# A hybrid decoder trunk in split single precision: first-half sum and second-half high parts moved at the changes of sub-layer

## What is computed

```python
def decoder_layer(x, state, norm_gains, ...):
    g = norm_gains
    x = x + 0.5 * rmsnorm(swiglu(rmsnorm(x, g[0]), ffn1_w_gate, ffn1_w_up, ffn1_w_down), g[1])
    mix, new_state = token_mixer(rmsnorm(x, g[2]), state, w_in, ..., w_out)
    x = x + rmsnorm(mix, g[3])
    x = x + 0.5 * rmsnorm(swiglu(rmsnorm(x, g[4]), ffn2_w_gate, ffn2_w_up, ffn2_w_down), g[5])
    return x, new_state
```

## Time and profile before

| | |
|---|---|
| Runs | 2288.12, 2284.45, 2284.33 us; median 2284.45 |
| Profiled execution | 2289.84 us, its span 2287.8 us |
| Mean granted TensorE clock | 0.986 of full speed |
| PE busy | 2223.0 us (97%), 19753 matmuls |
| DVE / ACT / POOL busy | 908.3 / 790.3 / 946.3 us |
| Chain that ended last | PE 92%, DVE 4%, ACT 2%, POOL 1%, issue 1% |
| DMA | 191.95 MB, 29.6% of the 16 engines' span |

### The profile page before, as it was taken

One profiled execution on the slowest core, in us unless ns is written; L12 is line 12 of the kernel. 1 busy time (PEld: TensorE's weight loads), 2 busy tenths in 40 slices (PEclk: granted clock), 3 DMA queues, 4 the chain that ended last, 5 costly groups with the idle time before them and its releaser, 6 DMA issues.

```text
span 2287.8 us, 45399 instructions
## 1 busy us (share of the span) xinstructions
PE 2223.0 (97%) x19753; PEld 2168.6 (95%) x19753; DVE 908.3 (40%) x1366; ACT 790.3 (35%) x1466; POOL 946.3 (41%) x781
## 2 busy tenths in 40 slices
PE   7999999999999999999999999999999999999998
PEld 7999999899888899999999999999998889999998
DVE  6333311666346733321263332135654556333113
ACT  4333322433343533332253333234143435333222
POOL 3644444433224444444444444434333344444442
PEclk9999999999999999999999999999999999999999
DMA  3333322322233233323223333323223132333232
GB/s 119 93 89 88 100 88 82 81 66 62 57 88 91 76 95 88 88 83 92 83 82 88 88 88 100 88 77 72 68 55 96 51 105 81 88 88 88 82 92 69
DMA packets 386181, 191.95 MB, mean 84 GB/s; under 512 B 31344, under 2 KB 384896, under 8 KB 385984
## 3 DMA queue, kind: packets, MB, share of 16 engines
q1 hardware_dynamic: 385984, 189.06, 29.6%
HBM read 180.26 MB, written 8.75 MB: 83 GB/s over the span
## 4 chain that ended last, share of the span: by engine, by line
PE 92%; DVE 4%; ACT 2%; POOL 1%; issue 1%; DMA 0%; SPq 0%; ACTq 0%
PE ps L771 84%; PE ps L993 1%; DVE xn_lo L1779 1%; DVE x L1793 1%; PE ps L1242 1%; POOL proj L755 1%; PE ps L929 1%; DVE numer L2169 0%; DVE y_ffn L1789 0%; ACT w_hi L1312 0%; DVE acc L1772 0%; ACT xn_hi L1323 0%; PE ps L1098 0%; PE ps L1139 0%; PE ps L1127 0%
## 5 line engine op out<-in xcount | busy, mean ns | idle before, releaser
L686 POOL TENSOR_TENSOR w_lo<-w_raw,w_hi 128x512 fp32r<-128x512 f32 (+1 forms) x680 | 881.9, 1301 | 1303.8 <-ACT w_hi L1312 1302.1
L771 PE MATMUL ps<-xn_hi,w_hi 128*128 128x272 f32 x3904 | 863.7, 295 | 32.3 <-DVE xn_lo L1779 25.2
L771 PE MATMUL ps<-xn_hi,w_lo 128*128 128x272 f32 x3904 | 846.9, 291 | 0.0
L771 PE MATMUL ps<-xn_lo,w_hi 128*128 128x272 f32 x3904 | 845.4, 290 | 0.0
L1312 ACT ACTIVATE w_hi<-w_raw 128x512 fp32r<-128x512 f32 (+1 forms) x680 | 415.1, 614 | 1073.8 <-PE ps L771 1018.8
L771 PEld LDWEIGHTS ps<-xn_hi,w_hi 128*128 128x128 f32 x3904 | 633.3, 191 | 57.8 <-DVE xn_lo L1779 31.4
L771 PEld LDWEIGHTS ps<-xn_lo,w_hi 128*128 128x128 f32 x3904 | 634.5, 191 | 0.2
L771 PEld LDWEIGHTS ps<-xn_hi,w_lo 128*128 128x128 f32 x3904 | 631.1, 191 | 0.0
L771 PE MATMUL ps<-h_hi,w_hi 128*128 128x272 f32 x1344 | 291.7, 288 | 0.0
L771 PE MATMUL ps<-h_lo,w_hi 128*128 128x272 f32 x1344 | 291.0, 287 | 0.0
L771 PE MATMUL ps<-h_hi,w_lo 128*128 128x272 f32 x1344 | 290.9, 287 | 0.0
(11 more groups left out here) (316 smaller groups left out, 1367.5 us busy)
## 6 DMA issues: line engine op xcount, KB each, us to landing
w_raw<-in_ffn_w_gate SPq DMA_DIRECT2D x168, 256.0 KB, 2.8
w_raw<-in_ffn_w_up SPq DMA_DIRECT2D x168, 256.0 KB, 2.8
w_raw<-in_ffn_w_down SPq DMA_DIRECT2D x160, 256.0 KB, 2.8
w_raw<-in_w_in SPq DMA_DIRECT2D x120, 256.0 KB, 2.8
w_raw<-in_w_out SPq DMA_DIRECT2D x32, 256.0 KB, 2.9
s_c<-in_state_mlstm_C SPq DMA_DIRECT2D x8, 512.0 KB, 6.1
out_c_s<-s_c SPq DMA_DIRECT2D x8, 512.0 KB, 5.9
tok_in<-in_x_prompt SPq DMA_DIRECT2D x4, 512.0 KB, 4.2
```

Source lines behind the costliest of these rows:

```text
L686: pool.tensor_tensor(w_lo[:, n % RING, 0:m], w_raw[:, n % RAW, 0:m], w_hi[:, n % RING, 0:m].bitcast(F32), ALU.subtract).then_inc(w_split, 1)
L771: mm = pe.matmul(pair(p)[:, a, :], w[:, q, ws], z[:, k, half(a)], start=(k == 0 and w is w_hi and z is hi), stop=(k == chunks - 1 and w is ...
```

## The change

Three edits, all of order; no instruction is added or removed.

```diff
@@ pe_ffn, closing: behind block 0 of the second half, no longer block 1
-                    if a == 1 and b == 1:
+                    if a == 1 and b == 0:
                         pe_post_sum(pe, v, 0)
@@ pe_mix, closing: inside the loop over blocks b, behind b == 0
+                        if a == 1 and t == DC - 3 and b == 0:
+                            pe_post_sum(pe, v, 0)
...
-                    if a == 1 and t == DC - 3:
-                        pe_post_sum(pe, v, 0)
@@ act_open
             act_x_square(act, 3)
+            act_x_high(act, v, 1, 5)
             act_high(act, n + 6)
-            act_x_high(act, v, 1, 5)
-            act_x_square(act, 4)
+            act_x_high(act, v, 1, 6)
             act_high(act, n + 7)
-            act_x_high(act, v, 1, 6)
-            act_x_square(act, 5)
             act_x_high(act, v, 1, 7)
             act_high(act, n + 8)
+            act_x_square(act, 4)
+            act_x_square(act, 5)
             keep_raw(1, 0)
@@ act_turn_from_ffn and act_turn_from_mix, the same edit in both
             act_high(act, n)
+            act_post(act, u, 0)
             act_high(act, n + 1)
-            act_post(act, u, 0)
```

## The result

| | before | with the change |
|---|---|---|
| Median | 2288.70 us (14 runs, 2284.33 to 2292.00) | 2278.11 us (14 runs, 2270.22 to 2282.57) |
| Ratio | | 0.9948, 95% interval 0.9939 to 0.9957 |
| Profiled execution | 2289.84 us, span 2287.8, mean granted clock 0.986 | 2282.23 us, span 2279.7, clock 0.986 |
| PE waits for a low part of x | 25.2 us, 22 times | 18.0 us, 14 times |

Faster by half a per cent, which the interval tells from no change; the forecast was 2276.0. The median of before over fourteen runs is 4.2 us above that of the three runs which the prediction had.

A forecast was written before the change was run, and what follows sets the result against it. PE, busy 97% of the span, idles 65 us; at the changes it waits for DVE's low part of x, held by POOL's splits. Terms of 9.9 us less idle: 2284.45 - 9.9 + 1.5 = 2276.0 us; range 2272 to 2279, with rivals 2271.5 to 2284.0.

The forecast's parts named there:

- rival B: At the three changes from an FFN POOL wins the 0.12 us tie: 2.7 us less won, 2278.7 us; chance 0.24.
- a split holds DVE off for about 1.05 us: POOL's split and a DVE operation on two SBUF tensors take turns, each split holding DVE off about 1.05 us.
- closing, three changes from an FFN: First halves after an FFN: earlier sum, Ln and Exp bring chunk 3's low part 1.1 us sooner each, 3.3 in all.
- closing, two from the mixer: First halves at the two changes that leave the mixer: the earlier sum wins 0.3 us each, 0.6 in all.
- opening, two with memsets: Second halves from FFN to mixer: memsets leave chunk 7's low part unheld, 1.9 us each, 3.8 in all.
- opening, the other three: Second halves of the other three changes: the split of n+7 holds chunk 7's low part; 0.6 us each, 1.8 in all.
- first opening: Opening of the first sub-layer: by the same reasoning as the other openings, 0.4 us won.
- rival E: The edits do nothing for PE because transfers or the ring are just behind: 2284 us; chance 0.06.
- I charge one more slow place, 1.5: Two pauses melted into one may slow more places to 1.2 GHz; 1.5 us added to the time.
- Rival D: Slower: melted pauses at six such places and two mixer first halves all run at 1.2 GHz, 2287.3 us; chance 0.09.
- the cover stays: Pre-norm sum in the openings: DVE still finishes about 2 us before PE asks for it.
- C (absorbed): DVE and POOL absorb the gain in first halves and openings without memsets; 4.2 us remain, 2280.3 us; chance 0.16.

The follow-up runs named there:

- The shorter splits: The whole change, but POOL splits only 128 of 512 columns of blocks n+1 to n+5 at each change; 2263.83 us, ratio 0.9875 to the kernel before.
- the last set of profiles: Kernel before, whole change, each edit by itself and a later-split order, together on another chip; before 2288.93 us, whole change 2277.33 us, ratio 0.9945.
- the opening alone: Kernel before with only the edit in `act_open`, closing as before; 2281.92 us, ratio 0.9959, and again 2283.16 us, ratio 0.9975.
- the split of n+7 later: Whole change plus chunk 7's high part and chunk 4's square moved before block n+7; 2274.67 us, ratio 0.9917, again 2274.19 us, 0.9931.
- the closing alone: Kernel before with only ACT's and PE's closing edits, `act_open` as before; 2285.84 us, ratio 0.9969, and again 2287.39 us, ratio 0.9989.

## Why the prediction was right, and where it wasn't

**The steps in the first half held.** "Chunk 3's starts at 407.7": moved by the 0.57 us by which the square came later in this profile, it starts at 407.71. "The second addition to x takes 1.3 us": 1.39. "One of about 2.0 us" for the melted pause: 1.87, at the first and third change. The tie of 0.12 us, on which rival B hung, went to DVE with 0.12 to spare, at the first and third change in every profile of this closing order. The shorter splits show the cause most directly.

**How long the hold lasts.** The prediction says that "a split holds DVE off for about 1.05 us". The hold has no length of its own: it lasts until the split ends. In the twelve profiles 427 of DVE's additions and low parts (128x272) start while a split is running, at least 0.1 us behind its start and 0.1 before its end. All but one of them end 0.30 us after that split does, to within 0.01, whether the split is long (412) or one of the short ones (14). So an operation loses up to 1.1 us, the more the earlier in the split it starts. The 1.05 served because in a row of splits each round takes 1.47 us, which is 1.05 more than DVE's own turn of 0.41. By the Trainium skill's page "SBUF — State Buffer" (SBUF: two separate sides) the hold lasts for the whole instruction; the traces agree. With splits in a row DVE still gets a turn between two: the two from 405.12 take 2.94 us, not 2.6.

**The terms, at full clock.** From the stretches of the last set of profiles, each edit's as the whole change against the other edit alone, at places at full clock (all but the fourth opening; the third, fourth and fifth change are read like the two shown). The first sub-layer's opening is read from DVE's last copy of x to the pre-norm sum, 24.30 us before and 23.86 with the change.

| term | forecast | measured |
|---|---|---|
| closing, three changes from an FFN | 3.3 | 1.09 + 1.05 + 0.46 = 2.6 |
| closing, two from the mixer | 0.6 | 0.18 + 0.17 = 0.35 |
| opening, two with memsets | 3.8 | 1.85 at the first, so 3.7 |
| opening, the other three | 1.8 | 0.73 + 0.68 + 0.52 = 1.9 |
| first opening | 0.4 | 0.44 |
| sum | 9.9 | 9.0 by position, 10.4 ± 0.9 by runs |

Each edit's own terms agree with its runs: closing 2.95 and 3.2 ± 0.8, opening 6.1 and 6.6 ± 0.8. For the whole change the runs give 1.4 us more than the places do, which is more than 0.9; what makes the rest was not found.

**One term was mis-sized: the closing of the fourth change.** The sum took the three changes from an FFN as one. ACT there, with the change:

```profile
1525.14 0.63 ACT L1312 ACTIVATE w_hi<-w_raw 128x512 fp32r<-128x512 f32 x1 [0.94 <-DMA w_raw<-in_w_in]
```

Block n+3 is now wanted 6.5 us after the square; at the fourth change its transfer lets it start only at 7.43, at the first it starts at 6.55. Before, ACT came to it at 7.82, so nobody saw the transfer. The splits of n+3 to n+5 then run in a row again, as in the earlier trace rows, and chunk 3's low part comes 13.82 us after the square, 0.43 sooner than before instead of 1.08. All profiles of this closing order show it at the fourth change (block n+3 starts 7.1 to 8.0 us after the square) and none elsewhere (at most 6.6). That is rival E in one place of five: the prediction checked block n+5's transfer and not those that the edit asks for earlier. The transfer is issued 3.60 us after the square at both; why it takes longer at the fourth change stays open. The two closings that leave the mixer were sized 0.3 each and gave about 0.17.

**"I charge one more slow place, 1.5" failed, and its sign was wrong.** The prediction held that pauses which melt into one long pause slow the clock more often. Counted over the eleven profiles with whole splits at all five changes, a place being slow if the work behind the pause took over 0.3 us longer than at full clock:

| pauses of PE, us | slow / places |
|---|---|
| FFN first half, 1.2 to 1.5 and 1.6 | 6 / 13 |
| FFN first half, one of 1.9 | 5 / 14 |
| second half, 1.3 and 0.8 or 1.0 | 6 / 20 |
| second half, one of 1.7 to 1.9 | 1 / 17 |
| second half, one of 0.7 to 0.9 | 0 / 18 |
| FFN first half, fourth change, 0.8 and 1.6 or 1.5 and 0.5 | 3 / 6 |
| mixer first half, 0.7 to 1.8 and 0.5 | 0 / 22 |

In the first halves the melting changes nothing that can be told; in the second halves two short pauses slow the clock in 6 of 20 and one pause, even a longer one than either, in 1 of 35. Two things limit the second count. Three of the six slow places lie in one profile, that of the kernel before. And five of the six follow a first half that was itself slowed: there two short pauses were slow in 5 of 8 places and one pause in none of 6, elsewhere in 1 of 12 and 1 of 29. So the difference rests on few places. Rival D falls by the time itself, which went down, and nothing here shows the clock taking more with the change. It gave: in the last set of runs the mean granted clock is 0.9888 with the whole change and 0.9874 before. The slow second halves before cost 10.0 us in those 20 places, 2.5 for five; the one of the 35 cost 1.6, which is 0.2 for five. The runs say about the same, though less surely: the two ratios of the whole change are 11.9 and 12.6 us of 2288.8, 1.5 to 2.2 more than the 10.4 at equal clock. But the opening alone, which has the same second halves, showed such a gain in one set (9.4 by ratio, 2.8 more than the 6.6 at equal clock) and none in the other (5.7), so its size is not settled. The Trainium skill's page "TensorE: Matmul & The Clock Gate" (Part 1) has the clock depend on recent activity and the count of slow matmuls vary from run to run; the runs agree with both, and show what that is worth here: 16 us between the fastest and the slowest of the 60 runs of before, at mean clocks of 0.991 and 0.983.

**Two errors cancelled in the predicted time.** The base of 2284.45 was a low draw: I took three runs for the median, which is 2288.70 over the 14 runs measured beside the change, 4.2 higher, and 2290.6 over the 60 others. "Most likely because fewer places ran slow" fits the fall of 1.8 us for each 0.001 of clock, but these three runs have no clock on record. From that base I took off 9.9 and put 1.5 back on for the clock, 8.4 in all, where the medians fell by 10.6. So the base was 4.2 too low and the gain 2.2 too small, and the time came out 2.1 too low. That it came so near is in part luck; the ratio tells it better: forecast 0.9963, measured 0.9948, below the forecast by more than its interval allows.

**Of the pre-norm sum, "the cover stays" was wrong at the changes to the mixer, at no cost seen.** DVE's sum over x in the first change, before and with the change:

```profile
428.61 6.78 DVE L1805 TENSOR_TENSOR acc<-acc,x_sq 128x544 f32<-128x544 f32 x6
```

```profile
423.61 10.48 DVE L1805 TENSOR_TENSOR acc<-acc,x_sq 128x544 f32<-128x544 f32 x6
```

It starts sooner and runs through the splits of n+7 and those behind it, which hold it. It ends at 434.09, and PE asks at 434.28. The cover of about 2 us that was forecast is 0.2 here and 1.3 at the fourth change; at the other three it is 2.0, as forecast. With the split of n+7 later it is 0.1 to 0.4 in 11 of 12 places. No profile shows PE waiting there, but an edit that holds this sum any longer would have to look at it.

**Rivals.** C (absorbed) falls: the closing alone wins 3.2 us, and openings without memsets win 0.5 to 0.7 each. E holds at one place. B's tie went to DVE wherever it arose; what the fourth closing lost (0.46 won instead of 1.1) comes near B's price, by another cause.

## What to carry to other kernels

When two engines hold each other off, price an earlier start by stepping both queues to the next thing that is waited for, and look for the order in which the waited-for operations come ahead of the holder: moving one weight block, and with it its split, behind the last low part was worth about as much as the whole closing edit (2.8 and 3.2 us, each give or take about 1). Check every transfer that an edit asks for earlier, at each place separately, not only the one that is late now. And where the clock varies from run to run, take the gain from places at full clock, or from many runs, compared at equal clock; one pair of profiles showed 15.4 us less in the changed stretches and 8.1 in the span.

## What the runs showed of the hardware

- A DVE operation on two SBUF tensors that meets a running split of POOL ends 0.30 us after the split does (426 of 427 in twelve profiles). A split of 128x512 (1.30 us) so costs it up to 1.1 us, one of 128x128 (0.47 us) up to 0.3: 0.56 us for an addition that takes 0.43 alone; the next two took 0.78 and 0.70 for 0.49 and 0.44. With splits in a row the two take turns.
- Memsets of POOL don't hold it: 30 additions and low parts that overlap only memsets take 0.43 and 0.49 to 0.50 us, as alone. Nor is a scaling of y held, which reads PSUM: 166 of them start within a split and take 0.42 to 0.44 us.
- The granted clock moves this kernel by 1.8 us for each 0.001; over 60 runs of one kernel it ran from 2284.83 to 2301.06 us.
- TensorE was slowed behind pauses of 1.3 and 0.8 to 1.0 us close together in 6 of 20 places, behind one of 1.7 to 1.9 in 1 of 17, behind one of 0.7 to 0.9 in none of 18. Five of the six followed a first half that had been slowed.
- One pause of 1.9 us slowed it in 5 of 14 first halves, one of 1.7 to 1.9 in 1 of 17 second halves. What differs between the two, the work ahead or behind, was not tried.
